# The gate stage of a streaming encoder in column groups of 512, with weight loads of 2 KB rows and two sets of PSUM banks

## The reference

```python
p = h @ w_in                       # w_in (2048, 8208): q, k, v, f, u, ga, gb
ga = p[..., OFF_GA:OFF_GB]         # OFF_GA = 4112, 2048 columns
gb = p[..., OFF_GB:IN_W]           # OFF_GB = 6160, 2048 columns
br_a = a_out @ w_attn_up           # attention branch, w_attn_up (1024, 2048)
br_b = (pooled per group @ w_pool) * pool_scale
m = sigmoid(ga) * br_a + sigmoid(gb) * br_b
x = x + rmsnorm(m @ w_out, g_mix_post)
h = rmsnorm(x, g_ffn_pre)
x = x + rmsnorm(square(relu(h @ w_ff1)) @ w_ff2, g_ffn_post)
```

## Time and profile before

| what | value |
|---|---|
| time of the runs, median of 3 | 1995.15 us (1991.63 to 1996.02) |
| span of the profiled execution | 1988.1 us (no other time of it is given) |
| PE busy | 1927.2 us, 97% |
| DVE, ACT, POOL busy | 843.4, 652.1 and 191.3 us (42%, 33%, 10%) |
| gate stage, pairs 1 to 7 | about 461 to 763 us of the span |
| granted PE clock, mean of the span | 0.992 |

### The profile page before, as it was taken

One profiled execution on the slowest core, in us unless ns is written; L12 is line 12 of the kernel. 1 busy time (PEld: TensorE's weight loads), 2 busy tenths in 40 slices (PEclk: granted clock), 3 DMA queues, 4 the chain that ended last, 5 costly groups with the idle time before them and its releaser, 6 DMA issues.

```text
span 1988.1 us, 27417 instructions
## 1 busy us (share of the span) xinstructions
PE 1927.2 (97%) x10576; PEld 1782.9 (90%) x10576; DVE 843.4 (42%) x1064; ACT 652.1 (33%) x896; POOL 191.3 (10%) x242
## 2 busy tenths in 40 slices
PE   5999999999999999996999999999999999999998
PEld 5999999889999998886989989899899898998996
DVE  6544444343433323336344443443444434434346
ACT  6334334343222323325323323223233232232332
POOL 0733333311110001001000000000000000000000
PEclk9999999999999999998999999999999999999999
DMA  9768889757787597332343443433434434334342
GB/s 172 150 145 184 188 174 122 199 133 132 104 135 134 114 85 253 128 126 83 122 144 116 138 128 114 139 115 124 141 115 137 128 113 140 117 123 140 116 136 98
DMA packets 231626, 268.68 MB, mean 135 GB/s; under 512 B 15314, under 2 KB 181426, under 8 KB 230545
## 3 DMA queue, kind: packets, MB, share of 16 engines
q1 hardware_dynamic: 216272, 235.98, 48.9%
q0 software_dynamic: 15296, 31.90, 5.3%
HBM read 260.69 MB, written 7.08 MB: 135 GB/s over the span
## 4 chain that ended last, share of the span: by engine, by line
PE 90%; DMA 7%; DVE 1%; ACT 1%; issue 0%; SPq 0%; DVEq 0%; ACTq 0%
PE ps L441 17%; PE ps L442 17%; PE ps L443 17%; PE ps L461 11%; PE ps L460 11%; PE ps L462 11%; DMA w_raw<-in_w_in_dram 7%; PE ps L595 1%; DVE w_lo L1183 1%; ACT w_hi L865 1%; PE ps L661 1%; PE ps L612 0%; PE ps L666 0%; PE ps L800 0%; PE ps L583 0%
## 5 line engine op out<-in xcount | busy, mean ns | idle before, releaser
L1183 DVE TENSOR_TENSOR w_lo<-w_raw,w_hi 128x1024 fp32r<-128x1024 f32 x438 | 543.1, 1264 | 573.8 <-ACT w_hi L865 573.6
L441 PE MATMUL ps<-ht_hi,w_hi 128*128 128x384 f32 x2064 | 697.6, 338 | 9.3 <-DVE w_lo L1183 7.6
L442 PE MATMUL ps<-ht_lo,w_hi 128*128 128x384 f32 x2064 | 691.0, 335 | 0.0
L443 PE MATMUL ps<-ht_hi,w_lo 128*128 128x384 f32 x2064 | 691.0, 335 | 0.0
L865 ACT CAST w_hi<-w_raw 128x1024 fp32r<-128x1024 f32 x438 | 450.3, 1049 | 655.1 <-PE ps L462 382.1
L441 PEld LDWEIGHTS ps<-ht_hi,w_hi 128*128 128x128 f32 x2064 | 388.3, 188 | 12.8 <-DVE w_lo L1183 8.9
L442 PEld LDWEIGHTS ps<-ht_lo,w_hi 128*128 128x128 f32 x2064 | 388.4, 188 | 0.5
L443 PEld LDWEIGHTS ps<-ht_hi,w_lo 128*128 128x128 f32 x2064 | 388.3, 188 | 0.0
L461 PE MATMUL ps<-w_lo,z_hi 128*128 128x512 f32 x768 | 302.6, 394 | 0.0
L460 PE MATMUL ps<-w_hi,z_hi 128*128 128x512 f32 x768 | 301.1, 392 | 1.0 <-DVE w_lo L1183 1.0
L462 PE MATMUL ps<-w_hi,z_lo 128*128 128x512 f32 x768 | 298.2, 388 | 0.0
(11 more groups left out here) (226 smaller groups left out, 1125.6 us busy)
## 6 DMA issues: line engine op xcount, KB each, us to landing
w_raw<-in_w_ff_dram SPq DMA_DIRECT2D x256, 512.0 KB, 4.1
w_raw<-in_w_in_dram SPq DMA_DIRECT2D x130, 512.0 KB, 9.1
w_raw<-in_w_out_dram SPq DMA_DIRECT2D x32, 512.0 KB, 4.0
kc<-in_cache_k_dram POOLq DMA_DIRECT2D x8, 1024.0 KB, 11.5
vc<-in_cache_v_dram POOLq DMA_DIRECT2D x8, 1024.0 KB, 10.7
w_raw<-in_w_attn_up_dram SPq DMA_DIRECT2D x16, 512.0 KB, 5.8
bias_s<-ncs_dram POOLq DMA_DIRECT2D x64, 48.0 KB, 6.3
out_dram<-z_gain SPq DMA_DIRECT2D x6, 512.0 KB, 2.7
```

Of the source, the lines that this page charges most:

```text
L441: pe.matmul(out, wh[:, k, cols], x_hi[:, kk, :], start=(kk == 0), stop=False)
L442: pe.matmul(out, wh[:, k, cols], x_lo[:, kk, :], start=False, stop=False)
L443: last = pe.matmul(out, wl[:, k, cols], x_hi[:, kk, :], start=False, stop=(kk == k_last))
L1183: nc.vector.tensor_tensor(w_lo[:, u % RING, :], w_raw[:, u % RING, :], f32(w_hi[:, u % RING, :]), ALU.subtract).then_inc(lo_ready, 1)
```

## The change

Pairs 0 and 1 stay as they are. The other twelve column tiles are now taken in three groups of 512 columns (`g` = 1 to 3, four tiles each, that is pairs 2g and 2g+1). A group has twenty units: eight of `ga`, eight of `gb`, four of the attention branch. Each unit is two k-tiles of 2 KB rows where it was four of 1 KB. The groups use two sets of four banks in turn, OUTER = 0, 1, 6, 7 and INNER = 2, 3, 4, 5: one set holds `ga` and later the branch, the other `gb`. Sigmoids go to buffers of their own for every tile (`sig_a`, `sig_b`, which lie where `mt_lo` and `mt_hi` will be), the sum is made in place in `brb`. The loop is written out. Because the sum now lies in `brb`, POOL's loads of `xres` wait until the last `mt_lo` is made. The first set of output units uses banks 3, 4, 5 and the second 0, 1, 2 (they were the other way round).

```diff
+    sig_b = place("sig_b", [P, KD, T], F32, R + 8 * KB)
+    sig_a = place("sig_a", [P, KD, T], F32)
...
+        OUTER, INNER = [0, 1, 6, 7], [2, 3, 4, 5]
...
-            with sp.Fori(0, 3) as i:
-                for j in range(2):
-                    gate_pair(U_GATE + 20 + 10 * j, i * 20, i * 2 + (2 + j))
+            for g in range(1, 4):
+                n = U_GATE + 20 * g
+                for q in range(8):
+                    load(n + q, 0, win(2 * q, 2, OFF_GA + 512 * g, 512), 2, 512)
+                for q in range(8):
+                    load(n + 8 + q, 0, win(2 * q, 2, OFF_GB + 512 * g, 512), 2, 512)
+                for q in range(4):
+                    load(n + 16 + q, 0, wup_v[:, 2 * q:2 * q + 2, 512 * g:512 * g + 512], 2, 512)
...
+            def gate_group(n, g):
+                mine, other = (OUTER, INNER) if g % 2 else (INNER, OUTER)
+                if g == 1:
+                    pe.wait_ge(ga_ready, 2)
+                else:
+                    pe.wait_ge(gb_ready, 2 * g)
+                for q in range(8):
+                    across(n + q, 0, 0, 4, 2 * q, 2, ht_hi, ht_lo, KD - 1, banks=mine)
+                if g == 1:
+                    pe.wait_ge(gb_ready, 2)
+                pe.wait_ge(ta_ready, 2 * g)
+                for q in range(8):
+                    across(n + 8 + q, 0, 0, 4, 2 * q, 2, ht_hi, ht_lo, KD - 1, banks=other)
+                pe.wait_ge(ga_ready, 2 * g + 2)
+                for q in range(4):
+                    across(n + 16 + q, 0, 0, 4, 2 * q, 2, at_hi, at_lo, PAIRS - 1, banks=mine)
...
-                        down(U_OUT + 8 * j + q, i * 16, [3 * j, 3 * j + 1, 3 * j + 2], 2 * q,
+                        down(U_OUT + 8 * j + q, i * 16, [3 - 3 * j, 4 - 3 * j, 5 - 3 * j], 2 * q,
...
+            def sigmoid_pair(g, h, side):
+                jp = 2 * g + h
+                banks = (OUTER if (g % 2) ^ side else INNER)[2 * h:2 * h + 2]
+                out = (sig_b if side else sig_a)[:, 2 * jp:2 * jp + 2, :]
+                nc.scalar.activation(out, ps[:, banks[0]:banks[0] + 2, 0:T],
+                                     ACT.Sigmoid).then_inc(gb_ready if side else ga_ready, 1)
...
+            def group_hi(jp):
+                act.wait_ge(m_ready, jp + 1)
+                nc.scalar.copy(mt_hi[:, 2 * jp:2 * jp + 2, :], brb[:, 2 * jp:2 * jp + 2, :]).then_inc(m_hi_ready, 1)
...
+            def group_gated(g, h):
+                jp = 2 * g + h
+                banks = (OUTER if g % 2 else INNER)[2 * h:2 * h + 2]
+                out = sig_a[:, 2 * jp:2 * jp + 2, :]
+                dve.wait_ge(ga_ready, jp + 1)
+                nc.vector.tensor_tensor(out, ps[:, banks[0]:banks[0] + 2, 0:T], out, ALU.mult).then_inc(ta_ready, 1)
...
+                for jp in (2 * g, 2 * g + 1):
+                    both = brb[:, 2 * jp:2 * jp + 2, :]
+                    pool.wait_ge(gb_ready, jp + 1)
+                    nc.gpsimd.tensor_tensor(both, sig_b[:, 2 * jp:2 * jp + 2, :], both,
+                                            ALU.mult).then_inc(tb_ready, 1)
+                for jp in (2 * g, 2 * g + 1):
+                    both = brb[:, 2 * jp:2 * jp + 2, :]
+                    pool.wait_ge(ta_ready, jp + 1)
+                    pool.wait_ge(tb_ready, jp + 1)
+                    nc.gpsimd.tensor_tensor(both, sig_a[:, 2 * jp:2 * jp + 2, :], both,
+                                            ALU.add).then_inc(m_ready, 1)
...
+            pool.wait_ge(m_lo_ready, KD // 2)
             for t in range(TT):
                 pool.dma_start(xres[:, t, :], xp_v[:, t, :] if t < 2 else xs_v).then_inc(xres_landed, 16)
-            pool.wait_ge(m_lo_ready, KD // 2)
             pool.dma_start(g_post_r[:, :], g_mix_post.broadcast_to([P, D])).then_inc(gpost_landed, 16)
```

More of the change, by code:

```diff
@@ L426, in unit, with across @@
                 return n % RING
-            def across(n, more, bank, tiles, k0, nk, x_hi, x_lo, k_last, parts=(0, 1)):
+            def across(n, more, bank, tiles, k0, nk, x_hi, x_lo, k_last, parts=(0, 1), banks=None):
                 slot = unit(n, more)
                 w = tiles * P
+                if banks is None:
+                    banks = [bank + c for c in range(tiles)]
                 wh = w_hi[:, slot, :].rearrange("p (k w) -> p k w", w=w)
@@ L437, in across @@
                     for c in range(tiles):
-                        out = ps[:, bank + c, 0:T]
+                        out = ps[:, banks[c], 0:T]
                         cols = slice(c * P, (c + 1) * P)
@@ L776, in _ @@
             gate_pair(U_GATE + 10, 0, 1)
-            with pe.Fori(0, 3) as i:
-                for j in range(2):
-                    gate_pair(U_GATE + 20 + 10 * j, i * 20, i * 2 + (2 + j))
-            pe.wait_ge(ga_ready, KD // 2)
+            def gate_group(n, g):
[14 more added lines that the diff above has]
+                    across(n + 16 + q, 0, 0, 4, 2 * q, 2, at_hi, at_lo, PAIRS - 1, banks=mine)
+            for g in range(1, 4):
+                gate_group(U_GATE + 20 * g, g)
             pe.wait_ge(gb_ready, KD // 2)
@@ L1531, in _, with group_lo @@
             gate_pair(U_GATE + 10, 0, 1)
-            with dve.Fori(0, 3) as i:
-                for j in range(2):
-                    gate_pair(U_GATE + 20 + 10 * j, i * 20, i * 2 + (2 + j))
-            merged_lo(7)
+            def group_gated(g, h):
[4 more added lines that the diff above has]
+                nc.vector.tensor_tensor(out, ps[:, banks[0]:banks[0] + 2, 0:T], out, ALU.mult).then_inc(ta_ready, 1)
+            def group_lo(jp):
+                dve.wait_ge(m_hi_ready, jp + 1)
+                nc.vector.tensor_tensor(mt_lo[:, 2 * jp:2 * jp + 2, :], brb[:, 2 * jp:2 * jp + 2, :],
+                                        f32(mt_hi[:, 2 * jp:2 * jp + 2, :]), ALU.subtract).then_inc(m_lo_ready, 1)
+            for g in range(1, 4):
+                n = U_GATE + 20 * g
+                slot(n, 0)
+                slot(n + 1, 0)
+                if g == 1:
+                    merged_lo(1)
+                    slot(n + 2, 0)
+                else:
+                    group_lo(2 * g - 2)
+                    slot(n + 2, 0)
+                    group_lo(2 * g - 1)
+                for q in range(3, 20):
+                    slot(n + q, 0)
+                dve.wait_ge(unit_used, n + 20)
+                group_gated(g, 0)
+                group_gated(g, 1)
+            group_lo(6)
+            group_lo(7)
             with dve.Fori(0, 2) as i:
@@ L1770, in _ @@
             store_rows(7)
-            with pool.Fori(0, KD // 2) as jp:
+            with pool.Fori(0, 2) as jp:
                 pool.wait_ge(gb_ready, jp + 1)
```

34 lines of the change are left out of this document (28 added, 6 removed).

## The result

The changed kernel takes 2005.44 us, the median of 5 runs (1999.7 to 2007.22), against 1995.15 us (5 runs, 1991.63 to 1996.1) for the kernel before: a ratio of 1.0049 [1.0035, 1.0064]. The numbers in brackets behind a ratio are its 95% interval. The forecast was 1987.1 us in a range of 1983.5 to 1997.5. The profiled execution took 2006.45 us, with a span of 2004.9 us against 1988.1.

What follows compares the result with a forecast made beforehand. The prediction took PE, busy for 97% of the span, to bound the kernel, with 10.3 us lost to weight waits in the gate stage. From 1995.15 us, -10.3 + 2.3 = -8.0 gave 1987.1 us, range 1983.5 to 1997.5.

Steps and rivals of the forecast that it cites:

- The loads and the stage, -10.3: Gate stage: mixing slow and ordinary columns in 2 KB rows ends PE's waits for weights, -10.3 us, bounds -10.3 and -8.3.
- The price that I took: Gate groups 1 and 3: each load of 2 KB rows costs 4.0 to 4.9 us, so PE does not wait.
- The end of the stage, +2.3: After the last branch unit: two pairs' sums and casts queue, PE waits 1.9 us plus restart; bounds +1.7 and +3.6.
- the 2.1 us that the prediction took: End of the stage: time of each of POOL's two sums, between 1.84 with DVE idle and 2.75 with DVE at work.
- POOL's transfers, 0: Behind the stage: `xres` goes out later, output unit 6's load wait moves about 4 us; costs nothing, at worst 1 us.
- Unrolling: Written-out gate loop: no cost, because pairs 0 and 1 are unrolled already and pair 1 runs at full pace.
- I read the slowness as one of place: Loads of pairs 3 and 7: slow (6.13 against 3.69 us) because of their columns, last quarter of 4 KB, not chance.
- A: Gate groups 1 and 3: 2 KB rows cost 5.1 to 5.3 us per load, about 10 us late, 1997 us; chance 0.15.
- B: Gate groups 1 and 3: whole 2 KB rows move at the slow rate, 6.13 us per load, 2028 us; chance 0.08.
- C: Stage end: longer queue, clock fall, transfer collision and loss partly absent in timed runs eat the gain, 1995 us; chance 0.12.

Runs made afterwards that it cites:

- e7: The changed kernel with the weight `w_in` declared first of the inputs, no instruction changed: 2022.67 us, ratio 1.0158.
- e13: The kernel before with PE's gate loop and head-pair loop both written out, nothing of the change: 1983.29 us, ratio 0.9947.
- e4: The changed kernel with ACT's small square root and its table load moved ahead of the last two casts: 2005.77 us, ratio 1.0051.
- e5: The kernel before with the gate loop written out on PE alone: 2014.53 us, ratio 1.0111.
- e6: The kernel before with the gate loop written out on SP, ACT and DVE but not PE: 1992.06 us, ratio 1.0004.
- e18: The kernel before with one feed-forward pass on PE written out ahead of its loop: 2007.54 us, ratio 1.0054.
- e16: The kernel before with three feed-forward passes on PE written out ahead of their loop: 1983.28 us, ratio 0.9939.
- e8: The changed kernel with a scratch tensor in DRAM made 512 bytes longer: 2004.07 us, ratio 1.0062.
- e1: The kernel before with the gate loop written out on SP, PE, ACT and DVE, nothing else of the change: 2013.85 us, ratio 1.0089.
- e2: The changed kernel, unaltered, run again: 2010.31 us, ratio 1.0084.
- e11: The changed kernel with ACT's table load ahead of the last two casts and PE's head-pair loop written out: 1985.48 us, ratio 0.9954.
- e14: The kernel before with PE's head-pair loop alone written out: 2019.13 us, ratio 1.0122.

## Why the prediction was wrong

- **The loads and the stage, -10.3: right.** Measured -10.36: 291.20 us in nine of the ten traces with the change, and no wait for weights in the three groups in any of the ten (e7's loss is in pair 1). The price that I took, 4.0 to 4.9 us per load, was too high: 3.2 to 3.5 by the windows. Nor is the price one of the row pitch or the columns alone: at the one pitch of 32,832 bytes the same columns moved at 91 to 92 GB/s (before), at 110 to 112 (e13, the same 1 KB rows) and, in 2 KB rows, at 151 to 165 in the two short windows above.
- **The end of the stage, +2.3: right in kind, mis-sized.** The PE wait was 1.22 instead of 1.9 us, the term 1.49 in all, under the lower bound of 1.7. The sums took 1.83 us each, though DVE was at work beside each of them for 0.8 to 0.9 us: its second product ended at 779.97, and the first difference began at 781.93. So the 2.1 us that the prediction took, a mean of the earlier trace rows by the time of DVE's work, was the part that was too long. e4 shows that it is this queue.
- **POOL's transfers, 0: right.** `xres` went out 2.2 us after the sums, behind the last difference; ACT's cast of output unit 6 waited for its load until 799.40, 3.8 us later against the stage's end than before, as forecast, and the rest of the program is no longer than the 1.49 us.
- **"Unrolling. Pairs 0 and 1 are unrolled already [...] so nothing": wrong, and this is the step that failed.** The measured price is +25.7 us in the profiled execution (an estimated 19 by the medians), all of it ahead of the stage. e5, e6 and e18 show that the longer PE program of these builds does it, on code that is the same and runs earlier. I had argued from the pace of unrolled code while it runs, and never asked what the rest of the program would do.
- **"I read the slowness as one of place": right, and not used.** The prediction took the place for a property of `w_in`. It is one of the build: the slow place moved by 512 bytes with the text, and the rate at it changed too. The 10.3 us that the change wins belong to the build as well: without the change, the stage took 300 to 305 us in eight traces, and 291.3 in e13 and e16. Where it takes 291.3, the change has nothing to win.
- **The rivals.** None of A, B and C names what happened. Their 1997 and 2028 us came from the stage's own loads, which were never late.

The sum by what was measured: -10.36 + 1.49 + 25.67 = +16.8 us of span; the timed medians differ by 10.3, for the reason given above. What the change is worth by itself depends on its surroundings. At 6040 matmuls it is up to 0.5%: 1.0111 [1.0094, 1.0128] for e5 and 1.0062 [1.0045, 1.0078] for e8 in one group, while e1 and e2 in another can't be told apart. At 6912 matmuls, e13 (without) and e11 (with) are at 0.9947 [0.9927, 0.9967] and 0.9954 [0.9933, 0.9975], not to be told apart (two groups, on two chips). The fastest kernels measured, e13 and e16 at 1983.3 us, are the kernel before with more of PE's program written out.

What stays open: by what path the text of PE's program reaches the loads. Shown as the cause is more text in PE's program, wherever it stands; the length alone doesn't give the size. Slower loads come with it (116 against 173 GB/s in one stretch of two builds, 92 against 110 in another), but e18's packets are quick and its start is late. Nor do the runs say why the slow head pair costs 2 to 5 us in e11, e13 and e16 and 13 to 18 in the late builds. That it goes by the place of tensors in memory fits the shift of the slow columns and the effect of declaring `w_in` first, but the addresses are in no trace, so it is not shown. One rival the traces speak against: that more text is fetched beside the loads. Up to the start of the stage the larger of the two queues that fetch instructions moved 15 packets in the kernel before, 15 in the changed one, 15 in e18 and e16, and 23 in both the late e14 and the early e13.

## What to carry to other kernels

Before you price a rewrite that also writes out a loop, run the unrewritten kernel with the loop written out: here that alone took 1.1% (e5) or 1.2% (e14) more time, 0.5% less (e13) or made no difference (e6), by what was written out. A gain that is read off slow transfers in one build belongs to that build, so compare a rewrite with a partner of the same program length, and split the span into what lies ahead of the edit, the edit and the rest. Wider rows of a load were a good insurance here: the three groups took 83.20 us each in all ten traces that had them, while with 1 KB rows the stage took anything from 291.3 to 305.

## What was new of the hardware

- The same instructions on the same data ran 10 to 33 us later at the same point when only text behind them had been added (starts of 471.20 in e16, 484.70 in e18, 484.71 in e5 and 494.24 in e1, against 461.28). Two builds were profiled twice and repeat their value within 3 us (461.28 and 461.15; 486.95 and 489.48), though the timed runs of one build spread more (2000.08 to 2016.23 for e18).
- Loads of 128 columns out of rows of 32,832 bytes have a slow place: in nine of the ten builds of the table 91 to 125 ns per packet of 512 bytes, against 34 to 81 elsewhere (e18: 72 against 38 to 50). The slow place moves by 512 bytes from build to build.
- PE's clock fell more often where PE waited more. Ahead of the stage it was granted 0.50 in one stretch of the kernel before, 6.8 us from 362.4, and in four of the changed kernel, from 151.8, 390.8, 401.0 and 421.5 us; this is the 1.2 GHz level. PE had stood still for a part of the time ahead of each: it was busy for 4.17 of the 6.40 us before 362.4, and for 3.06, 4.79 and 3.77 of the 6.80 us before 151.8, 390.8 and 401.0 and 10.17 of the 13.70 us before 421.5. e11, whose start is 3.6 us late, has no such stretch ahead of the stage. The one of before, then two of the changed kernel:

```profile
362.40:369.20 6.80, 4.98 (x41) 4.00 (x42) 2.83 (x4) 2.12 (x5) 0.21 (x1) 0.50 0.58 153
```
```profile
401.00:407.80 6.80, 5.98 (x26) 4.95 (x27) 2.77 (x8) 1.56 (x2) 1.17 (x1) 0.50 0.94 129
421.50:424.90 3.40, 3.40 (x17) 3.07 (x16) 0.00 (x0) 0.79 (x1) 2.89 (x6) 0.50 0.98 279
```
